# Paged attention in a four-layer decoder step: query broadcasts as single-pass products, ten key buffers, another order of page requests

## What is computed

```python
def moba_mixer(xn, pos0, w_qkv, w_o, k_pool, v_pool, li, table):
    q, k, v = jnp.split(xn @ w_qkv, 3, axis=-1)
    ...
    pool_sums = jnp.sum(k_pool[li], axis=1, dtype=jnp.float32)
    ...
    gate = jnp.einsum('blhd,bnhd->blhn', q.astype(jnp.float32), block_mean)
    ...
    _, sel = lax.top_k(gate, k_sel)
    ...
    s = jnp.einsum('bqhd,bqhkld->bqhkl', qg, kg).astype(jnp.float32) * scale
    s = jnp.where(mask, s, -jnp.inf).reshape(b, qb, H, n_slots * MOBA_BLOCK)
    p = jax.nn.softmax(s, axis=-1).reshape(b, qb, H, n_slots, MOBA_BLOCK).astype(vg.dtype)
    return jnp.einsum('bqhkl,bqhkld->bqhd', p, vg)
```

## Time and profile before

| | us |
|---|---|
| median of 3 runs | 1918.61 |
| profiled execution, device time | 1922.64 |
| its span | 1920.6 |
| qkv projection on PE ends | 642.4 |
| last key (63) begins on DVE | 749.7 |
| last value page used (quad(15)) | 792.7 |
| output projection of the attention begins | 800.3 |
| mean granted clock of TensorE | 0.955 |

### The profile page before, as it was taken

How to read it: one execution, slowest core, us unless ns; L and a number is a source line. 1 busy time by engine, 2 the same in 40 slices (tenths; PEclk the granted TensorE clock), 3 DMA queues, 4 the chain that set the end, 5 groups by cost and what they waited for, 6 DMA issues and landing times.

```text
span 1920.6 us, 35727 instructions
## 1 busy us (share of the span) xinstructions
PE 1777.6 (93%) x13503; PEld 1645.1 (86%) x13503; DVE 1302.6 (68%) x2434; ACT 957.7 (50%) x1738; POOL 507.7 (26%) x439
## 2 busy tenths in 40 slices
PE   8999989999999566899999979999999998999998
PEld 6998759999999422599999979999899875999997
DVE  6989795554576877365557875554899879655555
ACT  4456754553345756255434755433545676445333
POOL 2601401441130334154212234411160050144111
PEclk9999989999999766899999989999999998999999
DMA  7455474655567799765555446555546448365550
GB/s 215 153 176 159 141 233 133 206 175 177 174 237 272 277 370 411 282 207 187 174 172 160 154 129 209 176 166 171 156 133 194 137 132 263 122 211 184 176 175 23
DMA packets 317604, 365.05 MB, mean 190 GB/s; under 512 B 7738, under 2 KB 290562, under 8 KB 317382
## 3 DMA queue, kind: packets, MB, share of 16 engines
q1 hardware_dynamic: 296356, 288.46, 47.5%
q0 software_dynamic: 20944, 74.84, 10.4%
q10 hardware_dynamic: 176, 0.09, 0.0%
HBM read 340.79 MB, written 23.15 MB: 189 GB/s over the span
## 4 chain that ended last, share of the span: by engine, by line
PE 69%; DVE 17%; ACT 5%; issue 3%; DVEq 2%; DMA 2%; POOL 0%; POOLq 0%; ACTq 0%; SPq 0%
PE G L563 20%; PE G L564 20%; PE G L565 20%; DVE wlo L1767 4%; DVE sums L2092 3%; ACT whi L1094 2%; PE A L1030 2%; DVE xbc L1940 1%; PE A L524 1%; PE A L903 1%; DMA pg<-in_cache_k 1%; DVEq L1942 1%; DVE stx L2084 1%; PE G L524 1%; PE G L687 1%
## 5 line engine op out<-in xcount | busy, mean ns | idle before, releaser
L1767 DVE TENSOR_TENSOR wlo<-raw,whi 128x2048 fp32r<-128x2048 f32 x234 | 548.4, 2344 | 319.0 <-ACT whi L1094 318.9
L1094 ACT ACTIVATE whi<-raw 128x2048 fp32r<-128x2048 f32 x234 | 447.9, 1914 | 540.3 <-PE G L565 536.2
L563 PE MATMUL G<-xH,whi 128*128 128x264 f32 x2112 | 604.7, 286 | 14.0 <-DVE wlo L1767 11.4
L564 PE MATMUL G<-xH,wlo 128*128 128x264 f32 x2112 | 599.1, 284 | 0.0
L565 PE MATMUL G<-xL,whi 128*128 128x264 f32 x2112 | 598.8, 284 | 0.0
L563 PEld LDWEIGHTS G<-xH,whi 128*128 128x128 f32 x2112 | 398.4, 189 | 24.4 <-DVE wlo L1767 11.7
L564 PEld LDWEIGHTS G<-xH,wlo 128*128 128x128 f32 x2112 | 398.6, 189 | 0.4 <-issue 0.2
L565 PEld LDWEIGHTS G<-xL,whi 128*128 128x128 f32 x2112 | 396.7, 188 | 0.0
L563 PE MATMUL G<-aH,whi 128*128 128x264 f32 x1024 | 292.9, 286 | 8.0 <-DVE wlo L1767 8.0
L565 PE MATMUL G<-aL,whi 128*128 128x264 f32 x1024 | 291.5, 285 | 0.0
L564 PE MATMUL G<-aH,wlo 128*128 128x264 f32 x1024 | 291.4, 285 | 0.0
(11 more groups left out here) (473 smaller groups left out, 3098.3 us busy)
## 6 DMA issues: line engine op xcount, KB each, us to landing
raw<-in_mlp_w_up SPq DMA_DIRECT2D x64, 1024.0 KB, 5.3
raw<-in_mlp_w_down SPq DMA_DIRECT2D x64, 1024.0 KB, 5.1
raw<-in_ssd_w_in SPq DMA_DIRECT2D x48, 1024.0 KB, 5.4
pg<-in_cache_k POOLq DMA_DIRECT2D x64, 512.0 KB, 6.5
raw<-in_ssd_w_out SPq DMA_DIRECT2D x16, 1024.0 KB, 6.9
raw<-in_ple_w_gate SPq DMA_DIRECT2D x16, 1024.0 KB, 5.0
raw<-in_moba_w_qkv SPq DMA_DIRECT2D x12, 1024.0 KB, 7.1
pgw<-in_cache_v POOLq DMA_DIRECT2D x20, 512.0 KB, 6.8
```

Source lines behind the costliest of these rows:

```text
L563: mm(o, whi[u % 2][:, k, w], act_h[:, x, :], start=first, stop=False)
L564: mm(o, wlo[u % 2][:, k, w], act_h[:, x, :], start=False, stop=False)
L1094: fn(whi[u % 2][:], raw[(u + 2) % 4][:], ACT.Copy).then_inc(s_hi, 1)
L1767: V.tensor_tensor(wlo[u % 2][:], raw[(u + 2) % 4][:], whi[u % 2][:].bitcast(F32), ALU.subtract).then_inc(s_lo, 1)
```

## The change

It has three parts, all for layer 1.

- **Query broadcast.** `rows(0)` makes 16 transposes in place of 16 matmul instructions, and puts the 8 query rows on partitions 0 to 7 and again on 32 to 39. ACT copies all 40 rows rounded to fp32r into `rowQ`, DVE then writes the rest (query minus rounded query) into rows 32 to 39, behind its evacuation of chunk 4, and `query(n)` is two single-pass products of 512 columns over 40 rows. query(0) waits for the DVE step too.
- **Keys.** Two more buffers (`first_key`) hold keys 0 and 1; key t stands in buffer (t - 2) % 8, and keys 0 to 9 are requested without a wait. Seven in place of five are requested in `first_pages`, in layer 0.
- **Orders.** POOL requests values 8 to 11 into two of the `raw` buffers before key 22, when the last qkv chunk is split, and the later values two for three keys from key 26 on. On PE query(5), query(6) and query(7) come ahead of quads 1, 3 and 5, which stand one or two places later.

```diff
@@ -208,6 +208,9 @@
+        rowQ = at("rowQ", [40, D], m1 - 4 * D, F32R)
+        idq = at("idq", [40, NB], x1 + 5504, F32R)
+        first_key = [at(f"pgk{k}", [P, MH, P], 16 * TILE_B + 4 * MH * P * k)[:] for k in range(2)]
...
@@ -359,10 +363,15 @@
+        def key_slot(t):
+            if t < 2:
+                return first_key[t], s_kx, 32
+            return pg[f"pg{(t - 2) % 8}"][:], s_pg[(t - 2) % 8], 16 * ((t - 2) // 8 + 1)
+
-                return pg[f"pg{t - 48}"][:], s_pg[t - 48], 16 * (NB + 1)
+                return pg[f"pg{(t - 2) % 8}"][:], s_pg[(t - 2) % 8], 16 * (8 if t < 50 else 9)
...
@@ -800,21 +809,26 @@
                 def rows(j, dst):
                     for hh in range(MH):
-                        t_ = mm(dst[32 * j:32 * j + NB, hh // 4, (hh % 4) * P:(hh % 4 + 1) * P], qkv[:, 8 * j + hh, S_], ident[:], start=True, stop=True)
+                        o, w = slice((hh % 4) * P, (hh % 4 + 1) * P), qkv[:, 8 * j + hh, S_]
+                        if j == 0:
+                            tr(dst[0:40, hh // 4, o], qkv[:, hh, SEQ - 32:T], P)
+                            t_ = tr(dst[0:NB, hh // 4, o], w, P)
+                        else:
+                            t_ = mm(dst[32 + 32 * j:32 + 32 * j + NB, hh // 4, o], w, ident[:], start=True, stop=True)
                     t_.then_inc(s_rowT, 1)
                 def query(n):
                     if n >= 2:
                         pe.wait_ge(s_kd, PAGES * (n - 1 if n < 4 else n))
                     for c in range(2):
-                        t_ = mm(query_bank(n)[:, c, :], ident[0:NB, n:n + 1].to_broadcast([NB, P]),
-                                M["rowS"][0:NB, c * 512:(c + 1) * 512], start=True, stop=True)
+                        t_ = mm(query_bank(n)[:, c, :], idq[:, n:n + 1].to_broadcast([40, P]),
+                                rowQ[:, c * 512:(c + 1) * 512], start=True, stop=True)
                     t_.then_inc(s_qbc, 1)
                 def after_qkv(it, u):
                     r = it * 4 + u
                     if r == 4:
-                        pe.wait_ge(s_row, 1)
+                        pe.wait_ge(s_row, 2)
                         query(0)
                     if r == 5:
                         query(1)
...
@@ -921,22 +935,22 @@
                 front(1)
                 quad(0)
                 weights_T(1)
-                quad(1)
                 front(2)
                 head_sum(1)
+                query(5)
+                quad(1)
+                weights_T(2)
                 quad(2)
-                query(5)
-                weights_T(2)
-                quad(3)
                 head_sum(2)
                 front(3)
+                query(6)
+                quad(3)
+                weights_T(3)
                 quad(4)
-                query(6)
-                weights_T(3)
-                quad(5)
                 head_sum(3)
                 front(4)
                 query(7)
+                quad(5)
                 weights_T(4)
                 quad(6)
                 head_sum(4)
...
@@ -1294,14 +1308,22 @@
+                    if j == 0:
+                        fn(idq[0:32, :], ident[0:32, 0:NB], ACT.Copy)
+                        fn(idq[32:40, :], ident[32:40, 32:40], ACT.Copy)
-                    fn(M["rowS"][32 * j:32 * j + NB, :], src[32 * j:32 * j + NB].rearrange("b a n -> b (a n)"), ACT.Copy).then_inc(s_row, 1)
+                    if j == 0:
+                        fn(rowQ[:], src[0:40].rearrange("b a n -> b (a n)"), ACT.Copy).then_inc(s_row, 1)
+                    else:
+                        p = slice(32 + 32 * j, 32 + 32 * j + NB)
+                        fn(M["rowS"][p, :], src[p].rearrange("b a n -> b (a n)"), ACT.Copy).then_inc(s_row, 1)
+                    page, _, _ = key_slot(t)
-                        f = fn(pg[f"pg{j}"][:, hh, :], pg[f"pg{j}"][:, hh, :], ACT.Copy, accum_out=ms[f"sq{n % 2}"][:, j, hh:hh + 1])
+                        f = fn(page[:, hh, :], page[:, hh, :], ACT.Copy, accum_out=ms[f"sq{n % 2}"][:, j, hh:hh + 1])
...
@@ -1621,11 +1643,14 @@
-            def key_page(n, j):
-                if not (isinstance(n, int) and n == 0):
-                    pool.wait_ge(s_kd, n * PAGES + (j - 7))
-                    pool.wait_ge(s_ka, n * PAGES + (j - 7))
-                page(t_in["cache_k"], n * PAGES + j, pg[f"pg{j}"][:], s_pg[j])
+            def key_page(t, buf=None, landed=None, freed=None):
+                if buf is None:
+                    buf, landed, _ = key_slot(t)
+                    freed = t - 7 if t > 9 else None
+                if freed is not None:
+                    pool.wait_ge(s_kd, freed)
+                    pool.wait_ge(s_ka, freed)
+                page(t_in["cache_k"], t, buf, landed)
@@ -1640,33 +1665,35 @@
             def first_pages():
                 pool.wait_ge(s_load2, 16 * 13)
                 pool.wait_ge(s_mm, stage[0, "gate"]["g0"])
-                for j in range(5):
-                    key_page(0, j)
+                for t in range(7):
+                    key_page(t)
                 for t in range(3):
                     value_page(t)
             def moba():
                 qkv = stage[1, "qkv"]
                 pool.wait_ge(s_ev, qkv["c0"])
-                for j in range(5, PAGES):
-                    key_page(0, j)
+                for t in range(7, 10):
+                    key_page(t)
                 pool.wait_ge(s_xl, 16)
                 for t in (12, 13):
                     value_page(t)
                 pool.wait_ge(s_mm, qkv["g0"] + 2)
                 value_page(3)
-                with gp.Fori(1, 3) as it:
-                    for j in range(PAGES):
-                        key_page(it, j)
+                for t in range(10, 22):
+                    key_page(t)
+                pool.wait_ge(s_lo, stage[1, "wo"]["g0"])
+                for t in range(8, 12):
+                    value_page(t)
+                for t in range(22, 26):
+                    key_page(t)
                 pool.wait_ge(s_mm, qkv["g0"] + 12)
-                pool.wait_ge(s_lo, stage[1, "wo"]["g0"])
-                later = [t for t in range(4, NB * PAGES) if t not in (12, 13)]
-                for n in range(3, NB):
-                    for j in range(PAGES):
-                        key_page(n, j)
-                        if (PAGES * (n - 3) + j) % 3 < 2:
-                            value_page(later.pop(0))
-                    if n == 3:
+                later = [t for t in range(4, NB * PAGES) if not 8 <= t < 14]
+                for t in range(26, NB * PAGES):
+                    key_page(t)
+                    if t % 3 < 2:
+                        value_page(later.pop(0))
+                    if t == 31:
                         gp.memset(pm[:], 0.0).then_inc(s_const, 1)
                 for t in later:
                     value_page(t)
...
@@ -2172,7 +2199,12 @@
+                    if r == 8:
+                        dve.wait_ge(s_ka, 2)
+                    if r == 4:
+                        dve.wait_ge(s_row, 1)
+                        V.tensor_tensor(rowQ[32:40, :], A[0][32:40].rearrange("b a n -> b (a n)"), rowQ[32:40, :].bitcast(F32), ALU.subtract).then_inc(s_row, 1)
```

More of the change, by code:

```diff
@@ L189, in build_trunk @@
         ysp, _ = row(XT * TILE_B, [("yH", [P, XT, T], F32R), ("yL", [P, XT, T], F32R)])
[L191 removed]
+        M, m1 = row(0, [("qkv", [P, 3 * MH, T]), ("att", [P, KT, T]), ("spare", [P, 2 * D]), ("rowS", [104, D])])
         pg, m2 = row(m1, [(f"pg{j}", [P, MH, P]) for j in range(PAGES)])
@@ L2146, in key_scores @@
                     n, j = t // PAGES, t % PAGES
-                    page, q, sq = pg[f"pg{j}"], query_bank(n), ms[f"sq{n % 2}"]
+                    (page, landed, count), q, sq = key_slot(t), query_bank(n), ms[f"sq{n % 2}"]
                     if j == 0:
```

12 lines of the change are left out of this document (6 added, 6 removed).

## The result

The changed kernel takes **1931.75 us** (median of 4 runs, 1929.38 to 1932.38) against 1918.44 of the kernel before beside it: a ratio of **1.0067 [1.0050, 1.0084]** (in brackets the 95% interval). The profiled execution has 1931.15 us, a span of 1929.5 us, 8.9 more than before's 1920.6, and a granted clock of 0.954 (0.955 before).

A forecast was written before the change was run, and what follows sets the result against it. Page transfers were taken to bound layer 1's attention, through the arrivals of key 62 and value 63. Gains upstream were spent on transfers, leaving -0.5 us: 1922.64 to 1922.1, less 4.03 gives 1918.1 us; range 1912.0 to 1923.0.

The forecast's parts named there:

- Two more buffers, and values 8 to 11 earlier: Layer 1 requests: two more keys in layer 0 taken at nothing; earlier values save 2.9 us of DVE waits.
- 2.74 us of idle time ahead of value 63: POOL's unexplained wait late in the attention: if it stays, the end is 1.4 us later; the forecast leaned against that.
- Value 20: Its request on POOL in the attention: at 699.2 us, after some 11 us of standing for quad(1).
- Key 40: In the attention, behind query(5): begins at 696.0 us, 10.3 us earlier than before.
- Key 62: Its arrival in the attention: 749.6 us, 1.4 us later than before.
- Value 63: Its arrival late in the attention: 791.4 us, 1.3 us earlier than before.
- The end: End of the attention: between 1.4 us later and 1.3 earlier; leaning to the transfers, -0.5 us.
- The projection: Layer 1's qkv: cheaper query broadcasts evacuate the last chunk at about 640.3, -2.2 us; lower end 0, lost to DVE.
- Rival 2: Attention: POOL released later, value 20 requested at 702.8, key 62 5.0 us late; 1923.6 us; chance 0.21.
- Rival 1: Attention: POOL released earlier, value 20 requested at 695.0; about 1914 us, a gain of 4.7; chance 0.27.
- rival 3: Projection broadcasts were hidden anyway; value 20 requested at 701.4; about 1920.3 us, no change that can be told; chance 0.12.
- Late keys: DVE's waits in the attention: 2.9 us ahead of key 32 go, and waits return from key 43 on.

The follow-up runs named there:

- 15: Changed kernel with the requests of keys 8 and 9 behind those of values 12, 13 and 3, as in the kernel before; 1920.19 us, ratio 1.0019.
- 16: Kernel 10 with the requests of keys 8 and 9 ahead of values 12, 13 and 3; 1924.54 us, ratio 1.0042.
- Kernel 9: Kernel before with the new query broadcasts, and values 8 to 11 requested ahead of key 22; 1929.18 us, ratio 1.0068.
- kernel 1: Changed kernel with one POOL drain added right behind its last page request; 1921.72 us, ratio 1.0013.
- kernel 7: Kernel before with the new query broadcasts and two added POOL drains, behind value 3 and behind the last page request; 1919.51 us, ratio 0.9999.
- kernel 12: Kernel 10 with values 8 to 11 requested ahead of key 22; 1928.30 us, ratio 1.0053.
- 10: Changed kernel with the old orders on POOL and PE, leaving the query broadcasts and ten key buffers; 1916.95 us, ratio 0.9992.
- 4: Changed kernel with PE's old order of quads and queries; 1928.72 us, ratio 1.0058.
- 5: Changed kernel with five keys in place of seven requested in layer 0; 1930.57 us, ratio 1.0054.
- 14: Changed kernel with value pairs from key 24 on and none behind keys 39 and 40; 1930.31 us, ratio 1.0076.

## Why the prediction was wrong

**The failed step** is the one on "Two more buffers, and values 8 to 11 earlier", with the sum that is built on it. It prices the moved requests by their transfers alone, the requests of keys 8 and 9, which now go ahead of values 12, 13 and 3, have no term, and the sum ends with the start of wo. The range and every rival lay inside the attention. POOL's work behind its last request was thus put at nothing without a reason, and no row of POOL behind value 63 was read. Kernels 15 and 16 show that the place of the requests of keys 8 and 9 costs 7.6 to 7.8 us in the squares of the MLP, some 9 us in the whole kernel. A sign was there: the prediction names the 2.74 us of idle time ahead of value 63 "that no releaser explains" and bets, without a reason, that it goes. It went, which was luck, and the longer drain came with its going.

**The steps within the attention**, against the profile after:

- *Value 20* was forecast at 699.2 after some 11 us of waiting; it was 699.79 after 11.62. *Key 40*: 696.0, was 696.70. *Key 62*: 749.6, was 749.38. *Value 63*: 791.4, was 791.33. The gain at key 40 was spent on dry transfers, as forecast.
- *The end*: -0.5 us was forecast, -1.39 measured, of which layer 1 began 1.24 earlier. Within the layer it is -0.15.
- *Luck in these times*: the start of layer 1 lies anywhere from 565.8 to 572.2 us in the executions of this document. Counted from it, value 20 was requested at 129.2 us (forecast 127.4), key 62 came at 178.8 (177.8) and value 63 at 220.8 (219.6). The early start hides most of what the projection lost.
- *The projection*: -2.2 us was forecast, and 640.95 against 642.51 less that 1.24 leaves -0.3. The subtraction took 1.22 us (1.2 forecast) and PE waited 2.05. What was missing is PE's clock behind that wait: the window from 580 us has a granted clock of 0.91 (1.00 before), and PE's timeline shows the stretch at half clock (1.2 of 2.4 GHz), a product every 0.22 us and then every 0.12 again:

```profile
596.14 1.02 PE L824 MATMUL A<-rowQ,idq 40*128 40x512 f32 x2 [2.05 <-DVE rowQ L2207]
...
598.14 0.42 PE L573 MATMUL G<-xH,wlo 128*128 128x264 f32 x1
...
599.99 0.28 PE L573 MATMUL G<-xH,wlo 128*128 128x264 f32 x1
```

  The broadcast took 1.02 us where 0.5 was taken, and the 12 products behind it (597.10 to 599.87) 2.77 us in place of the 1.45 of the earlier trace rows: 0.5 + 1.3 = 1.8 us, the missing 1.9. The prediction had a bound of 0 for the term, but for another reason (DVE's work). Rival 2 names the row that shows such a stretch, half clock behind 2.04 us of standing, and says that PE will stand as long ahead of query(0), but it prices only quad(1) by it.
- *The rivals*: by the clock of the profile none came. Rival 1 wanted value 20 requested at 695.0, rival 2 behind 702 and rival 3 at 701.4. Counted from the start of layer 1, though, rival 3 puts value 20 at 129.6 us and it came at 129.2: the gain in the projection was lost, as rival 3 has it, but to PE's clock. Key 62 and value 63 came about halfway between rival 3 and the forecast.
- *Late keys*: the 2.9 us of waits ahead of key 32 are gone, and DVE waits 13.1 us for keys, all from key 43 on, both as forecast.
- The rule of the Trainium skill ("DMA: Bandwidth & Descriptors", "Anatomy of one DMA") that the issuing sequencer makes the wait held where it was used: what stands behind value 20 waits with it, 11.62 us here. Kernel 9 is a stronger case of it, with 17.52 us.

With the two requests back in place the changed kernel takes 1920.19 us. That is inside the range, but 0.19% [0.09, 0.28] slower than before beside it, where next to no change was forecast, and its attention is 2.6 us longer than before's, with the hold at value 63 back. So the forecast of the attention holds to within some 3 us, and what the sum lacked beyond that is a stage.

## What to carry to other kernels

- Moving a request changes more than when its page arrives. Read the moved engine's rows up to its next work in the following stage, and give that work a term or a bound, however far behind it lies.
- Where POOL drains behind many requests on a path that others wait on, put a drain into its idle time ahead: it gave back 10 us in kernel 1. In kernel 7, where the later drain was the short one, it gave nothing and cost nothing that can be seen.
- A request that waits for a buffer is placed by what releases it. Requests taken out ahead of it move it forward too, and everything behind it on the queue waits: four pages cost 16 us in kernel 9 and 10 in kernel 12.

## What the runs showed of the hardware

- POOL's drain in front of one addition stood for 2.45 to 2.62 us or for 9.31 us, never between unless a drain was added, and which of the two was set by the place of two requests some 245 us earlier (15 against the changed kernel, 16 against 10). In kernels 4, 5, 14 and 16 as in the changed one it is 9.31 each time.
- The short form goes with a hold of 2.1 us (2.69 to 2.74 less 0.62) at value 63's request, the long one with none. What POOL does in either, no row shows.
- A wait of 2.05 us of PE in a stage at full clock was followed by 3.7 us at half clock (596.14 to 599.87).
